# Weighting expert rows as they leave PSUM and summing the two results of a token in the scatter

## What is computed

```python
weights = (g_w[:, None] * top_p).reshape(-1)
expert = (g_idx[:, None] * EXPERTS_PER_GROUP + top_local).reshape(-1)
order = jnp.argsort(expert)
tok = order // TOP_K_INNER
xs = h[tok]
...
y = lax.ragged_dot(jax.nn.silu(a) * b, w2, sizes)
y = (y * weights[order][:, None]).astype(h.dtype)
...
# first_block, after the experts
x = x + gt2 * y
```

## Time and profile before

| | us |
|---|---|
| median of 3 runs | 3439.2 (3437.66 to 3440.77) |
| the profiled execution, its own time | 3440.75 |
| its span, first to last instruction | 3439.0 |
| PE busy in the span | 3171.2 (92%) |
| DVE busy | 2187.9 (64%) |
| ACT busy | 1311.9 (38%) |
| POOL busy | 1000.7 (29%) |

### The profile page before, as it was taken

The page is one execution under the profiler, slowest core; times in us unless marked ns, Lnnn a source line. Parts: engine busy times, 40 slices in busy tenths (PEclk is TensorE's granted clock), DMA queues, the critical chain, the costliest instruction groups (busy, mean ns, idle before and its releaser), DMA issues. The chain is left out here.

```text
span 3439.0 us, 44841 instructions
## 1 busy us (share of the span) xinstructions
PE 3171.2 (92%) x15137; PEld 2523.1 (73%) x15137; DVE 2187.9 (64%) x2685; ACT 1311.9 (38%) x1717; POOL 1000.7 (29%) x495
## 2 busy tenths in 40 slices
PE   5889989788899599999969999999799999999998
PEld 3657867455578488888847888888678888888877
DVE  5588886687643699999965876633465245245366
ACT  3245423566512288888843066201221000000142
POOL 1222433000043011111104443344234444444433
PEclk8999999899999699999989999999899999999999
DMA  6313211231042599999973122132221111111312
GB/s 228 78 44 92 79 51 31 86 118 56 32 170 71 196 372 379 380 380 380 382 288 104 55 79 91 46 118 81 95 77 48 49 44 49 49 49 49 110 37 68
DMA packets 351444, 446.15 MB, mean 130 GB/s; under 512 B 32942, under 2 KB 235612, under 8 KB 351332
## 3 DMA queue, kind: packets, MB, share of 16 engines
q1 hardware_dynamic: 336628, 410.08, 35.1%
q10 hardware_dynamic: 5344, 17.83, 1.6%
q0 software_dynamic: 9360, 16.80, 1.3%
HBM read 397.40 MB, written 58.75 MB: 133 GB/s over the span
## 5 line engine op out<-in xcount | busy, mean ns | idle before, releaser
L413 PE MATMUL acc<-Ah,whi 128*128 128x512 f32 x2336 | 932.1, 399 | 56.8 <-DVE Al L607 21.7
L414 PE MATMUL acc<-Al,whi 128*128 128x512 f32 x2336 | 916.1, 392 | 0.0
L415 PE MATMUL acc<-Ah,wlo 128*128 128x512 f32 x2336 | 915.6, 392 | 0.0
L385 POOL TENSOR_TENSOR whi<-wraw,one 128x1024 fp32r<-128x1024 f32 (+1 forms) x204 | 384.0, 1882 | 1783.5 <-PE acc L415 1465.4
L413 PEld LDWEIGHTS acc<-Ah,whi 128*128 128x128 f32 x2336 | 442.0, 189 | 178.2 <-issue 53.6
L387 POOL TENSOR_TENSOR wlo<-wraw,whi 128x1024 fp32r<-128x1024 f32 (+1 forms) x204 | 531.0, 2603 | 16.0
L414 PEld LDWEIGHTS acc<-Al,whi 128*128 128x128 f32 x2336 | 442.4, 189 | 96.2 <-issue 5.6
L415 PEld LDWEIGHTS acc<-Ah,wlo 128*128 128x128 f32 x2336 | 441.9, 189 | 94.4
L1864 DVE TENSOR_TENSOR mlo<-mraw,mhi 128x1024 fp32r<-128x1024 f32 x256 | 306.9, 1223 | 39.4 <-ACT mhi L1813 27.3
L1813 ACT ACTIVATE mhi<-mraw 128x1024 fp32r<-128x1024 f32 x256 | 267.8, 1062 | 81.5 <-PE acc L1758 50.3
L413 PE MATMUL acc<-Bh,whi 128*128 128x512 f32 x640 | 250.8, 392 | 8.3 <-POOL wlo L387 8.3
(11 more groups left out here) (511 smaller groups left out, 4772.8 us busy)
## 6 DMA issues: line engine op xcount, KB each, us to landing
mraw<-in_exp_w SPq DMA_DIRECT2D x512, 256.0 KB
mraw<-in_exp_w SPq DMA_DIRECT2D x128, 512.0 KB, 12.2
wraw<-in_w_in SPq DMA_DIRECT2D x72, 512.0 KB, 3.8
wraw<-in_w_up SPq DMA_DIRECT2D x48, 512.0 KB, 3.8
TT<-in_ada_w SPq DMA_DIRECT2D x32, 512.0 KB, 3.8
TT<-gates SPq DMA_DIRECT2D x32, 512.0 KB, 4.4
wraw<-in_w_down SPq DMA_DIRECT2D x24, 512.0 KB, 3.9
adaraw<-in_ada_w SPq DMA_DIRECT2D x16, 512.0 KB
```

Source lines behind the costliest of these rows:

```text
L385: ch(pool.tensor_tensor(whi[:, r, 0:k, 0:m], wraw[:, r, 0:k, 0:m], one[:, 0:1].unsqueeze(2).broadcast_to([P, k, m]), ALU.mult))
L413: pe.matmul(o, whi[:, r, j, 0:m], ih[:, k0 + j, cols], start=(j == 0), stop=False)
L414: pe.matmul(o, whi[:, r, j, 0:m], il[:, k0 + j, cols], start=False, stop=False)
L415: last = pe.matmul(o, wlo[:, r, j, 0:m], ih[:, k0 + j, cols], start=False, stop=(j == k - 1))
```

## The change

- `ys` of 2048 rows becomes `ysum` of 1024 rows, one for each token. SP fills it with zeros in the `wout` stage, by one transfer of 4 MB from a tile of 128 x 128 zeros (pieces of 512 B), behind the third weight load and ahead of the router's loads. POOL sets that tile at the start of the kernel.
- The scatter writes with `compute_op=ALU.add` to the token's row, so both experts' rows are added to one. Its index is `IDX`, which the gather uses too; `DST` is gone.
- The weight of each place is needed ahead of the scatter. DVE splits `WTOK` into three bf16 parts (`rW`) and makes `WEIGHT_AT`, 3 x 768 columns; 16 products with `PLACE` (144 columns each) and three small DVE operations give `WSLOT`, one weight for each place. ACT applies it in the copy out of PSUM (`scale=WSLOT[:, s]`).
- At the end SP reads eight transfers of 512 KB instead of 1 MB, `sum_rows` is gone, and PE's first `turn` waits for each read itself.

```diff
     def _(sp):
         for m in range(KD):
             load(sp, N0["wout"] + m, m % 2, WOUT[:, :, m * P:(m + 1) * P])
             if m == 2:
+                sp.dma_start(ysum.rearrange("(p a) (b n) -> p (a b) n", p=P, n=P),
+                             zeros[:].unsqueeze(1).broadcast_to([P, T * D // P // P, P])).then_inc(S("sum_zero"), 16)
                 sp.wait_ge(S("merged"), 8)
...
+        pe.wait_ge(S("routed"), 5)
+        for c in range(2 * NB):
+            last = pe.matmul(Y[:, HALF:HALF + 3 * (SLOTS + 1)], PLACE[:, c, :],
+                             WEIGHT_AT[:, c, :, :].rearrange("p a s -> p (a s)"), start=(c == 0), stop=(c == 2 * NB - 1))
+        last.then_inc(S("routed"), 1)
...
         dve.sem_inc(S("slot_rows"), 1)
+        weights = WTOK[:].rearrange("p k b -> p (k b)")
+        ch(dve.tensor_copy(rW[:, 0, :], weights))
+        ch(dve.tensor_tensor(rWf[:], weights, rW[:, 0, :], ALU.subtract))
+        ch(dve.tensor_copy(rW[:, 1, :], rWf[:]))
+        ch(dve.tensor_tensor(rWf[:], rWf[:], rW[:, 1, :], ALU.subtract))
+        ch(dve.tensor_copy(rW[:, 2, :], rWf[:]))
+        for i in range(3):
+            ch(dve.scalar_tensor_tensor(WEIGHT_AT[:, :, i, :], ROWAT[:, :, 0, :], 0.0,
+                                        rW[:, i, :].unsqueeze(2).broadcast_to([P, 2 * NB, SLOTS + 1]),
+                                        ALU.is_gt, ALU.mult))
+        dve.sem_inc(S("routed"), 1)
...
-            pool.indirect_dma_start(ys, bass.IndirectOffsetOnAxis(ap=IDD[:], axis=0), YO[:], None,
-                                    bounds_check=2 * T - 1, oob_is_err=False)\
+            pool.indirect_dma_start(ysum, bass.IndirectOffsetOnAxis(ap=IDD[:], axis=0), YO[:], None,
+                                    bounds_check=T - 1, oob_is_err=False, compute_op=ALU.add)\
...
-            act.activation(YO[:], acc[1][:], ACT.Copy).then_inc(S("y_out"), 1)
+            act.activation(YO[:], acc[1][:], ACT.Copy, scale=WSLOT[:, ds(s, 1)]).then_inc(S("y_out"), 1)
...
-            dve.tensor_copy(IDD[:], DST[:, ds(s, 1)]).then_inc(S("slot_dst"), 1)
+            dve.tensor_copy(IDD[:], IDX[:, ds(s, 1)]).then_inc(S("slot_dst"), 1)
...
+        ch(dve.tensor_copy(WSLOT[:], part(0)))
+        for i in range(1, 3):
+            ch(dve.tensor_tensor(WSLOT[:], part(i), WSLOT[:], ALU.add))
...
-            sp.dma_start(G12[:, :, b, :], ys.rearrange("(k b p) n -> b p k n", k=2, p=P)[b]).then_inc(S(f"y_in{b}"), 16)
-
-    @block.vector
-    def _(dve):
-        for b in range(3):
-            sum_rows(dve, b)
+            sp.dma_start(G[:, b, :], ysum[b * P:(b + 1) * P, :]).then_inc(S(f"y_in{b}"), 16)
...
-        for b in range(3, NB):
-            sum_rows(dve, b)
```

More of the change, by code:

```diff
@@ L244, in program @@
     rV = R("rV", [P, 1], 11808)
+    rW = R("rW", [P, 3, 2 * NB], 11840, BF16)
+    rWf = R("rWf", [P, 2 * NB], 11936)
+    WEIGHT_AT = alloc("WEIGHT_AT", [P, 2 * NB, 3, SLOTS + 1], BF16, offset=o_t + 4096)
     PLACE = alloc("PLACE", [P, 2 * NB, P], BF16, offset=o_ah)
@@ L254, in program @@
     IDX = small("IDX", [P, SLOTS + 1], I32)
-    DST = small("DST", [P, SLOTS + 1], I32)
+    WSLOT = small("WSLOT", [P, SLOTS + 1])
+    zeros = small("zeros", [P, P])
     IDC = small("IDC", [P, 1], I32)
@@ L273, in program @@
     HTl = alloc("HTl", [P, 4, P], F32R, offset=o_ah + 14336)
-    G12 = alloc("G12", [P, 2, NB, D], F32, offset=o_bl)
+    G = alloc("G", [P, NB, D], F32, offset=o_bl)
     RG = alloc("RG", [P, KD, T], F32, offset=o_bh)
@@ L308, in program @@
     h2rows = dram("h2rows", [T, D])
-    ys = dram("ys", [2 * T, D])
+    ysum = dram("ysum", [T, D])
     x2T = dram("x2T", [D, T])
@@ L445, in _ @@
         for t, v in ((one, 1.0), (eps, EPS), (ident, 0.0), (identb, 0.0), (causb, 0.0), (strict, 1.0), (onesb, 1.0),
-                     (meanD, 1.0 / D), (meanH, 0.0)):
+                     (meanD, 1.0 / D), (meanH, 0.0), (zeros, 0.0)):
             ch(pool.memset(t[:], v))
@@ L1638, in _ @@
         ch(dve.scalar_tensor_tensor(rSi[:], row_of, -1.0, rSi[:], ALU.add, ALU.add))
-        ch(dve.tensor_copy(DST[:], rSi[:]))
         ch(dve.tensor_scalar(rSj[:], rSi[:], float(T), -float(T), ALU.is_ge, ALU.mult))
@@ L1708, in _ @@
         pool.wait_ge(S("h2_st"), 16 * NB)
+        pool.wait_ge(S("sum_zero"), 16)
         def scatter(s):
@@ L1845, in _ @@
         slot(0, first=True)
+        act.wait_ge(S("routed"), 7)
         with act.Fori(1, end) as s:
@@ L1885, in _ @@
             low_up(0, q)
+        ch = chain(dve, "dve")
+        part = lambda i: Y[:, HALF + i * (SLOTS + 1):HALF + (i + 1) * (SLOTS + 1)]
+        dve.wait_ge(S("routed"), 6)
+        ch(dve.tensor_copy(WSLOT[:], part(0)))
+        for i in range(1, 3):
+            ch(dve.tensor_tensor(WSLOT[:], part(i), WSLOT[:], ALU.add))
+        dve.sem_inc(S("routed"), 1)
         def slot(s, first=False, last=False):
@@ L1911, in _ @@
         place(end)
[L1914 to L1920, removed]
     @block.sync
@@ L1925, in _ @@
         for b in range(NB):
-            sp.dma_start(G12[:, :, b, :], ys.rearrange("(k b p) n -> b p k n", k=2, p=P)[b]).then_inc(S(f"y_in{b}"), 16)
-    @block.vector
-    def _(dve):
-        for b in range(3):
-            sum_rows(dve, b)
+            sp.dma_start(G[:, b, :], ysum[b * P:(b + 1) * P, :]).then_inc(S(f"y_in{b}"), 16)
     stage.close()
-    lasting = [n for n in sems if n.startswith(("w_", "acc_free", "y_in")) or n in ("x1T_in", "y_sum", "act_step", "dve_step", "pool_step")]
+    lasting = [n for n in sems if n.startswith(("w_", "acc_free", "y_in")) or n in ("x1T_in", "act_step", "dve_step", "pool_step")]
     nc.clear_and_free_semaphores([sems[n] for n in sems if n not in lasting])
@@ L1994, in turn @@
             for b in range(NB):
-                last = pe.transpose(turn_banks[m % 2][:, b * P:(b + 1) * P], G12[:, 0, b, m * P:(m + 1) * P], ident[:])
+                if m == 0:
+                    pe.wait_ge(S(f"y_in{b}"), 16)
+                last = pe.transpose(turn_banks[m % 2][:, b * P:(b + 1) * P], G[:, b, m * P:(m + 1) * P], ident[:])
             last.then_inc(S("y_turned"), 1)
@@ L2000, in ahead @@
                 turn(j + 2)
-        pe.wait_ge(S("y_sum"), NB)
         turn(0)
```

## The result

| | before | after |
|---|---|---|
| median | 3438.8 us (4 runs, 3437.66 to 3440.77) | 3464.8 us (4 runs, 3463.34 to 3467.61) |
| the profiled execution | 3440.75 us, span 3439.0 | 3467.61 us, span 3463.9 |

The changed kernel takes 1.0076 times as long, with a 95% interval of 1.0063 to 1.0088: it is 26 us slower. The forecast was +11.3 us. Its sign and the range of 3427 to 3480 us hold the result; the 3446 to 3460 us that the forecast's own case gave itself do not.

The account below looks back on a forecast made before the run. The prediction took full DMA engines in the expert loop as the bound, plus the read at the block's end. Its terms, 20.9 + 1.0 + 0.3 + 0 - 10.9 = +11.3 us, gave 3450.5 us, range 3427 to 3480 us.

Parts of the forecast that it names:

- the forecast's own case: Whole kernel: added DMA time of 16 to 30 us, giving 3450.5 us, within 3446 to 3460; chance 0.40.
- What bounds the kernel: Expert loop: DMA engines are full, so added transfer work lengthens the loop nearly one for one.
- The scatter with an add: Expert loop: the add fetches 8.39 MB more, 0.70 us a slot for 30 slots, +20.9 us (bounds 0 and +42).
- The last scatter's landing: Behind the loop: fetching first delays the last scatter's landing by +1.0 us, between 0 and 3.1.
- rival d: Loop: scatter landing beyond 13.6 us makes DVE's `mlo` late, 42 us more, 3492 us; chance 0.08.
- The weights of places: Ahead of the loop: 3.8 us more DVE work, mostly covered by the first gather's wait; +0.3 us, at most +2.
- The zeros: Router stage: the 4.19 MB fill makes DVE wait some 4.5 us, still ahead of PE; 0, +3 at most.
- The end of the block: After the last scatter: the halved read ends sooner, then the wait for `wlo` sets the pace; -10.9 us.
- The sum: Whole kernel: all terms together give +11.3 us, 3450.5 us on the median.
- rival (c): Loop: the add costs twice the bytes, as the engine stalls between fetch and write; +42, 3471.6 us; chance 0.10.
- (a): Loop: the added read is hidden and only the block's end is felt, 3429.6 us; chance 0.20.
- (b): Loop: a part of the added read is hidden, 4 to 16 us, 3434 to 3446 us; chance 0.22.

Follow-up runs that it names:

- e1_plain: Changed kernel with a plain scatter in place of the adding one, so a token's later row overwrites the first; 3430.3 us, ratio to before 0.9978.
- e10: As e9_plain_light (one up-product pass left out), but with the add kept in the scatter; 3472.6 us.
- e5: Changed kernel with each slot's rows dealt evenly over all 128 places instead of packed into the first; 3460.8 us.
- e7_early: Changed kernel with the next block's first two weight tiles loaded, and the first split, ahead of the barrier; 3459.8 us.
- e4_half_plain: Changed kernel with a second, plain scatter per slot to a scratch tensor, for tokens below 512; span 3491.4 us (+27.5), one run.
- e3_empty_add: Changed kernel with a second adding scatter per slot that moves no row but token 0's; span 3467.9 us (+4.0), one run.
- e9_plain_light: Changed kernel without the add and with one of three passes of the expert's up product left out; 3449.1 us.

## Why the prediction was right, and where it was short

**What bounds the kernel: right.** The loop was said to take added DMA work nearly one for one. It does: without the add (e1_plain) the whole price goes, e10 shows the transfers as the bound with it, and ACT's waits for `mraw` from 1600 to 1740 us, forecast at some 30 us, are 31.0.

**The scatter with an add: right in kind, too small.** The step took the bytes once more, 20.9 us. The packets show that term, 19.8 us. The loop grew by 29.0 us, though. What the step left out, though it lies within its bounds of 0 and +42, are 3 to 4 us by which the weights' packets become longer, and some 7 us in which engines go short of work, of which an even deal wins a part (e5, 4.0 us in the time). So the slot is 19.1 us and not 18.7 to 18.8. The step turned bytes into time at a rate of 377 GB/s that the loop with the add does not keep: a slot's 6.82 MB (6.29 of weights, and 64 rows in the mean, gathered and scattered) took 18.08 us late in the loop before, 377 GB/s, and its 7.08 MB with the fetch take 19.08 us, 371 GB/s. That is 1.6% less, and 1.6% of 570 us is 9 us: a small loss on all bytes of the loop weighs nearly half as much as the price of the added ones, and the step looked only at these. Among its signs it named HBM reads, up by 8.4 - 4.2 MB; they fell by 4.2, as the page doesn't count the fetch.

**The last scatter's landing: +2.9, not +1.0.** Within the bound of 3.1 us that the text names, and nearly at it. In the records the 55 rows of this scatter run from 2.1 to 5.8 us after its issue, before from 1.6 to 2.9. They take 441 ns each in the mean and up to 1206, more than the 327 ns of the loop, though little else is moved then; why is open.

**Landing as a bound (rival d): right that it isn't one.** Scatters land in 9.4 us in the median, 11.2 at most, below the 13.6. DVE's index copies wait for POOL only at the last slots, 6.7 us in all (3.0 before).

**The weights of places: right.** The rows are where they were forecast:

```profile
1182.89 2.94 DVE L1663 SCALAR_TENSOR_TENSOR WEIGHT_AT<-ROWAT,rW 128x768 bf16<-128x768 bf16 x3
1186.93 6.90 DVE L1888 TENSOR_TENSOR mlo<-mraw,mhi 128x1024 fp32r<-128x1024 f32 x6 [1.10 <-ACT mhi L1836]
```

`mlo` was expected at about 1186.5 us. The first product of the loop starts at 1195.15 us, 0.44 later than before, for +0.3 forecast; 0.34 of it stood already at 1029 us, ahead of anything that the change touches in these stages, so about 0.1 is its price. PE's 16 products take 2.10 us in its wait.

**The zeros: 0 is right, by luck.** They land in 16.8 us (18.3 assumed). Yet DVE waited 7.5 us and not 4.5, for a reason that the step did not have. SP after:

```profile
1029.65 0.64 SPq L1340 DMA_DIRECT2D ysum<-zeros  x1
1030.33 13.23 SPq L1343 DMA_DIRECT2D rw<-in_router_w_grp  x1
1043.60 1.66 SPq L1344 DMA_DIRECT2D rw<-in_router_w_exp  x1
```

```profile
1050.95 0.31 DVE L1441 CAST rwh<-rw 128x288 fp32r<-128x288 f32 x1 [7.51 <-DMA rbias<-in_router_b_exp]
```

The next small load is held in SP's issue for 13.23 us (0.58 before) behind the 8192 pieces of the zeros: not only the data but the issue itself stands in line, and the fourth weight load is issued at 1046.84 us instead of 1033.44. Whether the number of pieces or the 4 MB hold it, no run tells. PE's product with the router's weights starts at 1052.76 us, for 1052.38 before, and DVE's split ends 1.0 us ahead of it. The step had put 3.2 us on that split, by its 3.1 us before; it took 0.8 (0.31 + 0.46). With 3.1 it would have ended 1.3 us behind PE, so nothing came of the wait only because another term came out smaller.

**The end of the block: -8.4, not -10.9.** The text gives the last step to this number, through the third and fourth tile, without its working. The read was said to be done 12.65 us after its issue; the last transpose that waits for it starts 14.6 us after. PE starts on the first blocks only behind the barrier, at 1820.47 us, and takes the rest at the reads' pace of 1.29 us, as forecast. The weights land at 1829.61 us, 16.4 us after the read's issue and not 14.4. POOL's `wlo` takes 3.41 us and not 2.36, with DVE's split (L611, 1.28 us) beside it; in e7_early, where DVE stands idle, it takes 2.34. The step named the wait for `wlo` as the late one, and e7 shows that it was: without it 4.9 us are won. e1_plain gains it too: from the read's issue (1776.80 us) to the last `C` (1813.65) it is 36.9 us there, 9.3 less than before, in a kernel that is 8.4 us faster.

**The sum.** 29.0 + 0.6 + 2.9 - 8.4 against 20.9 + 0.3 + 1.0 - 10.9 (loop, what lies ahead of it, last landing, end): short by 8.1, 0.3, 1.9 and 2.5 us, all on one side. The result of 3464.8 us lies 14 us above the forecast of 3450.5, outside the 3446 to 3460 us that it gave itself, and only 7 us under rival (c), the doubled price of 3471.6 us. Rival (c)'s mechanism, an engine that takes three times as long for a row, falls with the packets, which take twice as long. That the range of 3427 to 3480 us holds is thus owed to its width, which took this rival in; the sign and the way to it were forecast. Rivals (a) and (b), the hidden read, fall with e1_plain: of 19.8 us of engine time nothing was hidden.

## What to carry to other kernels

Where the DMA engines are full, a scatter that adds costs at least twice a plain one in engine time (327 and 159 ns for a row of 4 KB), and here 34.5 us of the kernel for 8.39 MB that would take 22 us as bytes; by these figures it can pay only where the engines have slack or where the read that it saves is longer, which no run here tried. Look for such work in the share of the packets' time for a queue, not in its bytes or in HBM reads, where an add's fetch does not appear. And where a queue is full, price a transfer by more than its packets: 1024 more plain rows held the engines for 10 us and lengthened the loop by 22. When a read at a barrier is made shorter, follow what is queued behind it first: 4.9 us, more than a third of the gain that was to be had, stood behind a weight load that could have been issued earlier.

## What the runs showed of the hardware that was not expected

- An adding row packet of 4 KB takes a DMA engine 327 ns, a plain one 159 ns, and the page's counters of bytes don't show the fetch (393.21 MB read from HBM with the add and without).
- A load that follows a transfer of 8192 pieces of 512 B in SP's queue was held in its issue for 13.23 us.
- A second scatter for each slot, plain, of 1024 rows in all, took 10 us of engine time and made the loop 22 us longer (e4_half_plain against e3_empty_add, one run each).
- POOL's issue of a gather or scatter took 1 to 2 us in most slots and 4.62 and 9.37 us in every second slot of e9_plain_light, beside DVE operations of two inputs without a pause. That kernel, with less work for PE, was 19 us slower than e1_plain, and its DVE waited for POOL in those slots.
- 4096 places of a scatter with hardly a row in them cost about 4 us, in one run.
